# A fused attention and expert layer on one core: routing loop reordered, one index DMA per block

## The chip, the cores and the metric

One Trainium2 chip (trn2), one core of it. The metric is the device time of one execution in microseconds (us), taken from unprofiled runs; the kernel's time is their median. A profiled execution was taken beside them; all views of the trace come from that one.

## What is computed

One decoder layer on 1024 tokens of width 1024, all float32: RMS norm, one combined projection, sliding-window and differential attention, gates, an output projection added to the input, and then a sparse expert network. The part that matters here, from the attention's end on:

```python
x = x + mixed @ w_o
xn = rms_norm(x, ffn_norm_g)
logits = xn @ router_w + router_b              # 1024 tokens, 32 experts
top_vals, top_idx = top_k(logits, 4)
gates = softmax(top_vals)
# each token goes to its 4 experts:
h = xn @ w1[e] + b1[e]                          # w1[e] is 1024 x 2048
g, u = split(h); g = min(g, 7); u = clip(u, -7, 7)
y = (g * sigmoid(1.702 * g) * (u + 1)) @ w2[e] + b2[e]   # w2[e] is 1024 x 1024
x = x + sum over the 4 experts of gate * y
out = rms_norm(x, final_norm_g)
```

## The kernel before

The first 886 us are the attention half; the diff doesn't touch it. The expert half has two stages and a short end.

**Routing (lines 1026 to 1155 on VectorE, 1217 to 1273 on PE, 957 to 980 on ACT, 905 to 914 on POOL).** The 1024 tokens are 8 tiles of 128 (NT = 8). For each tile PE makes the output product in two halves of 512 columns, each 8 products of 128x128 by 128x512 (`out_product`, L1251); VectorE adds them to the input (`residual`, L1052); ACT sums the squares and takes the root (`norm_rms`, L963 and L965); VectorE scales (`norm`, L1065); PE transposes the tile (`turn_xn`, L1224), and ACT and VectorE copy the two halves out of PSUM (`store_xn`, L971 and L1075). PE makes the logits (L1237), VectorE finds the best four and a 0/1 mask (`best`, L1080 to L1093), ACT the exponentials (L975), PE counts the tokens ahead of each in each expert, over all tiles so far (`rank`, L1243), and VectorE turns this into positions (`place`, L1098 to L1107). POOL then scatters, in 4 indirect DMAs per tile, each token's number and gate to its position in a DRAM table of slots, `slot_rows`, where a row has 8 bytes (L912). SP stores the residual and the normalised rows to DRAM.

The order is written out by hand on each engine as a loop over rounds t, each step lagging by a number of rounds. On PE a round is: both halves of tile t, transposes of t-1, logits of t-2, rank of t-3. ACT's exponentials and VectorE's `place` lag four rounds, `best` three. The lists of blocks are computed after the last rank (L1126 to L1155), and end in `list_ready`. SP issues the loads of w2 of expert 0 and of half of w1 of expert 1, 8 MB, after the last tile is stored (L859 and L862).

**Experts.** The slots are cut into blocks of 32 token rows, each of one expert; there are 145 blocks. A block's 32 rows are held in four groups of 32 partitions, each with a quarter of the columns. ACT loads the block's 32 slot rows (`load_slots`, L988) into all four groups of partitions of `idxa`, in four DMAs on its own queue, asked for several blocks ahead, one pair of semaphores `idx_in` for even and odd blocks. POOL adds the group number (L920) and gathers the token rows with an indirect DMA (`gather`, L923), VectorE transposes (L1190), PE makes the product with w1 (`up`, L1283; four k-tiles from `reg_r`, which VectorE copies there for each block, L1183, and four from `w_hi`), VectorE and ACT the activation (L1165 to L1173, L994), PE the product with w2 (`down`, L1306), ACT weighs the rows (L1000), POOL adds them into DRAM (`scatter`, L933). In a block's round ACT does the sigmoid of block n, weighs block n-1 and then issues the index DMAs of block n+4.

SP loads weights as they come free, in loads of 1 MB: when the last block of an expert has used the upper half of w1, the four loads of the next expert's (L868), then the w2 loads (L873) when w2 has been used, and the lower half of w1 of the expert after that (L877).

At the end the rows are read back, normalised and stored.

Of the kernel before, what the change touches and what calls it, by code (L numbers as in the profile page):

```python
# [10 lines left out]
ALU = mybir.AluOpType  # L11
ACT = mybir.ActivationFunctionType
# [686 lines left out]
def expert_half(nc, a, tabs_s, reg_h, reg_r, x_back):  # L699
# [11 lines left out]
    with ExitStack() as ctx:  # L711
# [72 lines left out]
        nb, end_c, count = sm[0:32, 204:205], sm[0:32, 205:206], sm[0:32, 206:207]  # L784
        ntop, exs, rexs = sm[:, 208:216], sm[:, 216:224], sm[:, 224:232]
# [118 lines left out]
        def _(pool):  # L904
# [10 lines left out]
            def gather(n, b, half, reused):  # L915

                pool.wait_ge(idx_in[b], half * 64 + 64)
# [38 lines left out]
        def _(act):  # L956
# [15 lines left out]
            for t in range(NT + 4):  # L972
                if t >= 4:
                    act.wait_ge(top_ready, t - 3)
                    act.activation(ex[:, t - 4, :], top[:, t - 4, 0:TOPK], ACT.Exp, bias=ntop[:, t - 4:t - 3],  # L975
                                   accum_out=exs[:, t - 4:t - 3]).then_inc(ex_ready, 1)
                if t < NT:
                    norm_rms(t)
                if 1 <= t <= NT:
                    store_xn(t - 1)  # L980

            def load_slots(n, b, half):

                if not (isinstance(half, int) and half == 0):
                    act.wait_ge(idx_in[b], half * 64)
                row = act.value_load(listi[0:1, 1, bass.ds(n, 1)], min_val=0, max_val=TABROWS - QB)
                for j in range(NG):
                    act.dma_start(idxa[QB * j:QB * j + QB, bass.ds(n, 1), :].rearrange("p o v -> p (o v)"),  # L988
                                  tab_d[bass.ds(row, QB), :]).then_inc(idx_in[b], 16)
# [28 lines left out]
            act.wait_ge(idx_in[0], n_iters * 64 + 192)  # L1018
            act.wait_ge(idx_in[1], n_iters * 64 + 128)
# [7 lines left out]
        def _(dve):  # L1027
# [17 lines left out]
            def residual(t):  # L1045

                if t == 0:
                    dve.wait_ge(x_back, 16)
                for half in range(2):
                    v = x2[:, t, half * 512:(half + 1) * 512]  # L1050
                    dve.wait_ge(o_proj, 2 * t + half + 1)
                    dve.tensor_tensor(v, v, bank[2 + half][:, :], ALU.add).then_inc(x2_done, 1)  # L1052
# [58 lines left out]
            for t in range(NT + 4):  # L1111
                if 1 <= t <= NT:
                    norm(t - 1)
                if 2 <= t <= NT + 1:
                    store_xn(t - 2)
                if 3 <= t <= NT + 2:
                    best(t - 3)
                if t >= 4:
                    place(t - 4)
                if t < NT:  # L1120
                    residual(t)
# [95 lines left out]
        def _(pe):  # L1217
# [10 lines left out]
            def logits(t):  # L1228
# [5 lines left out]
                if t >= 2:  # L1234
                    pe.wait_ge(rank_taken, t - 1)
# [4 lines left out]
            def rank(t):  # L1240
                pe.wait_ge(mask_ready, t + 1)
                for s in range(t + 1):
# [3 lines left out]
            def out_product(t):  # L1246
                for half in range(2):
                    if t:
                        pe.wait_ge(x2_done, 2 * t - 1 + half)
                    for k in range(KD):  # L1250
                        ins = pe.matmul(bank[2 + half][:, :], mixT[:, k, t * P:(t + 1) * P], wo_s[:, k, half * 512:(half + 1) * 512],  # L1251
                                        start=(k == 0), stop=(k == KD - 1))
                    ins.then_inc(o_proj, 1)
            for t in range(NT + 3):
                if t < NT:
                    out_product(t)
                if 1 <= t <= NT:
                    turn_xn(t - 1)
                if 2 <= t <= NT + 1:
                    logits(t - 2)  # L1260
                if t >= 3:
                    rank(t - 3)
# [89 lines left out]
```

## Time and profile before

| | |
|---|---|
| median of 3 runs | 3001.46 us (2997.08 to 3006.98) |
| profiled execution, its own time | 3002.64 us |
| its span, first to last instruction | 3000.8 us |
| mean granted TensorE clock | 0.931 of full speed |
| busy: PE, VectorE (DVE), ACT, POOL | 88%, 49%, 12%, 24% of the span |
| bytes moved | 499.22 MB in 166005 packets |

A profile page gives each engine's busy time, the span in slices, the DMA queues (q1 is SP's, q10 ACT's, q0 POOL's), the chain of work that ended last, and the costliest groups of instructions, each with the idle time of the engine before it and what ended that. Questions to the trace give the same for a stretch: its instructions in order of time, the DMA packets in it, busy times and granted clock. "L1283" is a line of the kernel. Names such as `reg_r<-in_w` say what is written from what.

### The profile page before, as it was taken

Reading aid. Unit: us, or ns where it says so; the run is one execution under the profiler, and the core shown is the slowest. Engines: PE = TensorE matmul, PEld = TensorE weight load, DVE = VectorE, ACT = ScalarE, POOL = GpSimd, SP = SyncE. Lnnn points to the kernel's source line nnn. Section 1 sums busy time; section 2 is a strip of 40 time slices with the busy share of each in tenths; the row PEclk is TensorE's granted clock in tenths of the full one; section 3 lists DMA queues with packets and bytes.
Section 4 is the critical chain, followed back from the end, with each engine's and each line's share of the span. In section 5 each row is a group of like instructions: output and inputs, shape, how many; then the busy total and the mean of one; then the engine's idle time right before and its main releaser. Section 6 shows DMA issues by size and latency. Waiting matters only on the chain.

```text
span 3000.8 us, 63110 instructions
## 1 busy us (share of the span) xinstructions
PE 2642.1 (88%) x22972; PEld 1187.1 (40%) x22973; DVE 1481.6 (49%) x2879; ACT 364.6 (12%) x870; POOL 724.8 (24%) x623
## 2 busy tenths in 40 slices
PE   8999988899998868799999989899889879997755
PEld 4644666444444422244433424234333323332212
DVE  4342787201114445466666656565555546664334
ACT  2001554100001200000000000000000000000002
POOL 0000000000000323244444424244334333442112
PEclk9998798899999879899999989999999999998878
DMA  3100000500025478731556283935786775579993
GB/s 134 56 28 1 1 1 1 154 28 21 21 86 173 143 245 320 255 119 26 191 179 200 71 306 106 363 113 176 258 296 211 242 273 186 189 249 368 378 355 133
DMA packets 166005, 499.22 MB, mean 166 GB/s; under 512 B 46032, under 2 KB 82384, under 8 KB 132944
## 3 DMA queue, kind: packets, MB, share of 16 engines
q1 hardware_dynamic: 108176, 459.96, 40.8%
q0 software_dynamic: 29168, 38.39, 6.7%
q10 hardware_dynamic: 28608, 0.19, 0.5%
q8 instruction: 29, 0.48, 0.1%
q14 instruction: 24, 0.20, 0.0%
HBM read 466.64 MB, written 32.15 MB: 166 GB/s over the span
## 4 chain that ended last, share of the span: by engine, by line
PE 41%; DMA 26%; issue 1%; SPq 1%; DVE 1%; ACT 0%; DVEq 0%; ACTq 0%; POOLq 0%; POOL 0%
PE xbank L1283 24%; DMA w_hi<-in_w 17%; PE xbank L1306 13%; DMA reg_r<-in_w 9%; PE xbank L1251 3%; PE xbank L1293 1%; PE xbank L1300 0%; DVE reg_h L1213 0%; PE xbank L1237 0%; DMA w_hi<-in_b 0%; SPq L868 0%; DMA reg_h<-acc_rows 0%; PE xbank L1224 0%; SPq L877 0%; DMA acc_rows<-stage,idxs 0%
## 5 line engine op out<-in xcount | busy, mean ns | idle before, releaser
L1183 DVE COPY reg_r<-reg_r 128x2048 f32 x580 | 678.5, 1225 | 467.4 <-DMA reg_r<-in_w 219.5
L1283 PE MATMUL xbank<-reg_r,stage 128*32 128x512 f32 x4640 | 572.5, 630 | 102.6 <-DVE reg_r L1183 81.0
L1306 PE MATMUL xbank<-reg_r,stage 128*32 128x256 f32 x9280 | 561.3, 391 | 79.8 <-DMA reg_r<-in_w 79.4
L1283 PE MATMUL xbank<-w_hi,stage 128*32 128x512 f32 x4640 | 555.2, 613 | 58.4 <-DMA w_hi<-in_w 58.3
L1306 PEld LDWEIGHTS xbank<-reg_r,stage 128*32 128x32 f32 x9280 | 312.5, 113 | 318.1 <-DMA reg_r<-in_w 103.4
L933 POOL DMA_INDIRECT acc_rows<-stage,idxs x145 | 340.9, 2351 | 120.9 <-POOL idxs L930 110.0
L1283 PEld LDWEIGHTS xbank<-reg_r,stage 128*32 128x32 f32 x4640 | 157.9, 114 | 427.6 <-issue 277.1
L1283 PEld LDWEIGHTS xbank<-w_hi,stage 128*32 128x32 f32 x4640 | 153.5, 112 | 393.4 <-issue 261.7
L930 POOL TENSOR_TENSOR idxs<-idxa,tok 128x1 int32<-128x1 int32 x145 | 28.8, 199 | 971.1 <-ACT stage L1000 940.0
L531 PE MATMUL pair<-reg_r,reg_h 128*128 128x512 f32 (+1 forms) x640 | 253.2, 551 | 0.3 <-DMA reg_r<-in_w_in 0.3
L923 POOL DMA_INDIRECT stage<-xn_rows,idxg x147 | 192.8, 1311 | 121.5 <-POOL idxg L920 113.0
L994 ACT ACTIVATE stage<-stage 128x256 f32<-128x256 f32 x145 | 60.5, 417 | 1297.5 <-DVE stage L1165 978.2
L905 POOL DMA_DIRECT2D bcs<-order_table x1 | 0.8, 756 | 886.3 <-POOLq L86 886.3
L920 POOL TENSOR_TENSOR idxg<-idxa,tok 128x1 int32<-128x1 int32 x147 | 205.7, 1400 | 14.5 <-DMA idxa<-slot_rows 13.3
L531 PEld LDWEIGHTS pair<-reg_r,reg_h 128*128 128x128 f32 x640 | 119.3, 191 | 114.6 <-issue 110.5
L1190 DVE STREAM_TRANSPOSE stage<-stage 128x256 f32<-128x256 f32 x147 | 63.1, 429 | 183.9 <-DMA stage<-xn_rows,idxg 183.8
L1000 ACT ACTIVATE stage<-xbank,idxa 128x256 f32<-128x256 f32 x145 | 68.4, 472 | 472.6 <-PE xbank L1306 453.2
L1251 PE MATMUL xbank<-reg_r 128*128 128x512 f32 x256 | 114.2, 605 | 9.4 <-DVE reg_h L1052 7.5
L648 PE MATMUL pair<-reg_h,reg_ka 128*128 128x512 f32 x256 | 114.3, 606 | 4.2 <-DMA reg_r<-in_w_diff_out 4.2
L648 PE MATMUL pair<-reg_h,reg_g 128*128 128x512 f32 x256 | 111.2, 592 | 0.0
L1165 DVE TENSOR_SCALAR stage<-xbank 128x256 f32<-128x256 f32 x145 | 61.4, 423 | 70.5 <-PE xbank L1283 70.3
L283 ACT ACTIVATE reg_r<-pair,small 128x256 f32<-128x256 f32 (+7 forms) x128 | 76.8, 600 | 114.4 <-DVE small L417 58.2
(187 smaller groups left out, 1959.8 us busy)
## 6 DMA issues: line engine op xcount, KB each, us to landing
reg_r<-in_w SPq DMA_DIRECT2D x256, 1024.0 KB
w_hi<-in_w SPq DMA_DIRECT2D x128, 1024.0 KB, 5.6
idxa<-slot_rows ACTq DMA_DIRECT2D x596, 0.2 KB
reg_r<-in_w_in SPq DMA_DIRECT2D x4, 2048.0 KB, 7.9
reg_r<-in_x SPq DMA_DIRECT2D x8, 512.0 KB, 3.4
reg_ka<-in_w_in SPq DMA_DIRECT2D x8, 512.0 KB, 3.8
reg_g<-in_w_in SPq DMA_DIRECT2D x8, 512.0 KB, 3.9
reg_r<-in_w_o SPq DMA_DIRECT2D x1, 4096.0 KB, 17.1
```

The costliest lines, as they stand in the source:

```text
L283: act.activation(probs[u % 2][c][:, 0:n], pair[c][:, 0:n], ACT.Exp, bias=nm[:, s:s + 1], scale=ATT_SCALE, accum_out=lsum[:, s:s + 1]).then ...
L531: ins = pe.matmul(bank[n % 2][:, 0:w], hT[:, k, t * P:(t + 1) * P], wv[:, k, :], start=(k == 0), stop=(k == KD - 1))
L648: ins = pe.matmul(bank[br][:, :], wv[:, k, :], hT[:, k, tok], start=(k == 0), stop=(k == KD - 1))
L920: pool.tensor_tensor(idxg[b][:, :], idxa[:, bass.ds(n, 1), 0], group, ALU.add).then_inc(idxg_ready, 1)
L923: pool.indirect_dma_start(out=xg[b], out_offset=None, in_=xn_parts, in_offset=bass.IndirectOffsetOnAxis(ap=idxg[b][:, :].bitcast(U32), axi ...
L933: pool.indirect_dma_start(out=acc_parts, out_offset=bass.IndirectOffsetOnAxis(ap=idxs[b][:, :].bitcast(U32), axis=0), in_=yrow[b], in_offs ...
L1000: act.activation(yrow[b], y_bank[b][:, 0:DG], ACT.Copy, scale=gate_a[:, bass.ds(n, 1), 1]).then_inc(y_taken, 1)
L1183: dve.tensor_copy(w1k[k], lo_from[:, bass.ds(slot, 1), k, :].rearrange("p o n -> p (o n)")).then_inc(w1_filled[k], 1)
L1190: dve.transpose(xT[b], xg[b]).then_inc(xT_ready, 1)
L1251: ins = pe.matmul(bank[2 + half][:, :], mixT[:, k, t * P:(t + 1) * P], wo_s[:, k, half * 512:(half + 1) * 512], start=(k == 0), stop=(k == ...
L1283: ins = pe.matmul(up_bank[b][QB * c:QB * c + QB, :].rearrange("p (h k q) -> p h k q", h=2, q=QB), xT[b][:, QB * k:QB * k + QB], w1k[k].rea ...
L1306: ins = pe.matmul(y_bank[b][QB * j:QB * j + QB, 0:DG], actT[b][:, QB * k:QB * k + QB], w2r[:, k, j * DG:(j + 1) * DG], start=False, stop=( ...
```

## The change

Three edits, all in the expert half.

*Order of the routing loops.* On PE a round is now: first half of tile t's output product, logits of t-2, second half, transposes of t-1, rank of t-2. `logits` waits for the mask of two tiles before (`mask_ready`), and `rank` has the wait for `rank_taken` that `logits` had. On VectorE a round is: `norm` of t-1, first residual add of t, `best` of t-2, second add, copy of t-1, `place` of t-2. ACT's exponentials lag two rounds. All loops are one or two rounds shorter.

*Square root.* After each exponential of rounds 2 to 7 ACT takes one square root of a constant into a spare column.

*Index loads.* `load_slots` issues one DMA for all four groups, whose source is the 32 rows with a repeated outermost dimension of 4, and the counts that are waited for go by 16 instead of 64.

```diff
+        root_c = sm[:, 207:208]
...
-                pool.wait_ge(idx_in[b], half * 64 + 64)
+                pool.wait_ge(idx_in[b], half * 16 + 16)
...
-            for t in range(NT + 4):
-                if t >= 4:
-                    act.wait_ge(top_ready, t - 3)
-                    act.activation(ex[:, t - 4, :], top[:, t - 4, 0:TOPK], ACT.Exp, bias=ntop[:, t - 4:t - 3],
-                                   accum_out=exs[:, t - 4:t - 3]).then_inc(ex_ready, 1)
+            for t in range(NT + 2):
+                if t >= 2:
+                    act.wait_ge(top_ready, t - 1)
+                    act.activation(ex[:, t - 2, :], top[:, t - 2, 0:TOPK], ACT.Exp, bias=ntop[:, t - 2:t - 1],
+                                   accum_out=exs[:, t - 2:t - 1]).then_inc(ex_ready, 1)
+                    if t < NT:
+                        act.activation(root_c, eps_c, ACT.Sqrt)
                 if t < NT:
                     norm_rms(t)
...
-                    act.wait_ge(idx_in[b], half * 64)
+                    act.wait_ge(idx_in[b], half * 16)
                 row = act.value_load(listi[0:1, 1, bass.ds(n, 1)], min_val=0, max_val=TABROWS - QB)
-                for j in range(NG):
-                    act.dma_start(idxa[QB * j:QB * j + QB, bass.ds(n, 1), :].rearrange("p o v -> p (o v)"),
-                                  tab_d[bass.ds(row, QB), :]).then_inc(idx_in[b], 16)
+                act.dma_start(idxa[:, bass.ds(n, 1), :].rearrange("p o v -> p (o v)"),
+                              tab_d[bass.ds(row, QB), :].unsqueeze(0).to_broadcast([NG, QB, 2])).then_inc(idx_in[b], 16)
...
-            def residual(t):
+            def residual(t, half):
...
-            for t in range(NT + 4):
+            for t in range(NT + 2):
                 if 1 <= t <= NT:
                     norm(t - 1)
-                if 2 <= t <= NT + 1:
-                    store_xn(t - 2)
-                if 3 <= t <= NT + 2:
-                    best(t - 3)
-                if t >= 4:
-                    place(t - 4)
                 if t < NT:
-                    residual(t)
+                    residual(t, 0)
+                if t >= 2:
+                    best(t - 2)
+                if t < NT:
+                    residual(t, 1)
+                if 1 <= t <= NT:
+                    store_xn(t - 1)
+                if t >= 2:
+                    place(t - 2)
...
             def logits(t):
...
                 if t >= 2:
-                    pe.wait_ge(rank_taken, t - 1)
+                    pe.wait_ge(mask_ready, t - 1)
...
             def rank(t):
                 pe.wait_ge(mask_ready, t + 1)
+                if t >= 2:
+                    pe.wait_ge(rank_taken, t - 1)
...
-            for t in range(NT + 3):
+            for t in range(NT + 2):
                 if t < NT:
-                    out_product(t)
+                    out_product(t, 0)
+                if t >= 2:
+                    logits(t - 2)
+                if t < NT:
+                    out_product(t, 1)
                 if 1 <= t <= NT:
                     turn_xn(t - 1)
-                if 2 <= t <= NT + 1:
-                    logits(t - 2)
-                if t >= 3:
-                    rank(t - 3)
+                if t >= 2:
+                    rank(t - 2)
```

## Rows read from the trace of the kernel before

**Rows 1.** The chain that ended last, on the page: shares of the span.

```profile
PE 41%; DMA 26%; issue 1%; SPq 1%; DVE 1%; ACT 0%; DVEq 0%; ACTq 0%; POOLq 0%; POOL 0%
...
PE xbank L1283 24%; DMA w_hi<-in_w 17%; PE xbank L1306 13%; DMA reg_r<-in_w 9%; PE xbank L1251 3%; PE xbank L1293 1%; PE xbank L1300 0%; DVE reg_h L1213 0%; PE xbank L1237 0%; DMA w_hi<-in_b 0%; SPq L868 0%; DMA reg_h<-acc_rows 0%; PE xbank L1224 0%; SPq L877 0%; DMA acc_rows<-stage,idxs 0%
```

**Rows 2.** Busy us (count) of PE, PEld, DVE, ACT, POOL; granted clock, DMA share, GB/s.

```profile
940.00:1020.00 80.00, 80.00 (x278) 42.04 (x278) 29.81 (x103) 19.70 (x35) 15.38 (x16) 1.00 0.40 119
...
1030.00:1035.00 5.00, 3.00 (x20) 2.89 (x19) 2.87 (x14) 0.39 (x2) 3.18 (x4) 0.50 1.01 407
```

**Rows 3.** The chain in order of time: start us, us, what.

```profile
1029.45 20.21 DMA reg_r<-in_w
...
1049.66 19.98 issue
...
1069.64 5.31 PE xbank L1283 x32
```

**Rows 4.** Timeline of the tail: start us, us, engine, line, operation [idle before].

```profile
1021.72 1.87 PE L1237 MATMUL xbank<-rw,stage 128*128 128x32 f32 x16
...
1022.97 1.28 ACT L965 ACT_TABLE_LOAD   x1
...
1024.90 1.67 DVE L1065 SCALAR_TENSOR_TENSOR stage<-reg_h,sm,stage 128x256 f32<-128x256 f32 x4
...
1029.24 3.60 PE L1237 MATMUL xbank<-rw,stage 128*128 128x32 f32 x16 [0.64 <-DVE row_of L1098]
...
1034.42 0.37 DVE L1093 TENSOR_REDUCE maskb<-hot 128x32 bf16<-128x128 f32 x1
...
1043.69 0.17 DVE L1107 CAST posi<-sm 128x4 int32<-128x4 f32 x1
```

**Rows 5.** Timeline of POOL: first and last scatter of tile 7.

```profile
1047.39 0.95 POOL L912 DMA_INDIRECT slot_rows<-tok,posi  x1 [0.30 <-issue]
...
1051.17 0.96 POOL L912 DMA_INDIRECT slot_rows<-tok,posi  x1 [0.31 <-issue]
```

**Rows 6.** DMA packets of 1030 to 1036 us (first row) and 1036 to 1062 us.

```profile
DMA packets 660, 2.45 MB, mean 408 GB/s; under 512 B 64, under 2 KB 64, under 8 KB 659
...
DMA packets 1517, 5.72 MB, mean 220 GB/s; under 512 B 639, under 2 KB 639, under 8 KB 1005
...
q0 software_dynamic: 544, 0.02, 1.5%
```

**Rows 7.** Timeline of ACT's queue and POOL at the first blocks.

```profile
1062.02 9.25 ACTq L988 DMA_DIRECT2D idxa<-slot_rows  x16
...
1065.25 0.18 POOL L920 TENSOR_TENSOR idxg<-idxa,tok 128x1 int32<-128x1 int32 x1 [12.00 <-DMA idxa<-slot_rows]
```

**Rows 8.** Costliest groups, on the page: busy us, mean ns, idle us before.

```profile
L994 ACT ACTIVATE stage<-stage 128x256 f32<-128x256 f32 x145 | 60.5, 417 | 1297.5 <-DVE stage L1165 978.2
```

**Rows 9.** DMA of 1078 to 1082, 1082 to 1090 (two rows), 1476 to 1480, 1480 to 1484.

```profile
DMA packets 217, 1.65 MB, mean 412 GB/s; under 512 B 16, under 2 KB 16, under 8 KB 16
...
DMA packets 578, 2.77 MB, mean 346 GB/s; under 512 B 240, under 2 KB 240, under 8 KB 240
...
q10 hardware_dynamic: 192, 0.00, 1.2%
...
DMA packets 419, 1.60 MB, mean 399 GB/s; under 512 B 29, under 2 KB 29, under 8 KB 419
...
DMA packets 472, 1.11 MB, mean 278 GB/s; under 512 B 201, under 2 KB 201, under 8 KB 472
```

**Rows 10.** SP's queue from 898 to 899 us, and the router load's issues (ns).

```profile
q1 hardware_dynamic: 365, 0.05, 29.3%
...
L836 SPq DMA_DIRECT2D rw<-in_router_w x8: 532/532/5161, 890.5 to 899.3; - x8
```

**Rows 11.** The chain's DMA pieces over 10 us, first and last of 50.

```profile
1078.81 11.23 DMA w_hi<-in_w
...
2914.55 11.41 DMA reg_r<-in_w
```

More of the change, by code:

```diff
@@ L1017, in _ @@
             weigh_y(n_iters * 2, 0)
-            act.wait_ge(idx_in[0], n_iters * 64 + 192)
-            act.wait_ge(idx_in[1], n_iters * 64 + 128)
+            act.wait_ge(idx_in[0], n_iters * 16 + 48)
+            act.wait_ge(idx_in[1], n_iters * 16 + 32)
             for t in range(NT):
@@ L1043, in split_bias @@
                 return dve.tensor_copy(parts[64:96, :], whole[64:96, :])
-            def residual(t):
-                if t == 0:
+            def residual(t, half):
+                if t == 0 and half == 0:
                     dve.wait_ge(x_back, 16)
[L1049 to L1052, printed above, removed]
+                v = x2[:, t, half * 512:(half + 1) * 512]
+                dve.wait_ge(o_proj, 2 * t + half + 1)
+                dve.tensor_tensor(v, v, bank[2 + half][:, :], ALU.add).then_inc(x2_done, 1)
             def norm(t):
@@ L1244, in rank, with out_product @@
                 ins.then_inc(rank_done, 1)
[L1246 to L1253, printed above, removed]
-            for t in range(NT + 3):
-                if t < NT:
-                    out_product(t)
+            def out_product(t, half):
+                if t:
+                    pe.wait_ge(x2_done, 2 * t - 1 + half)
+                for k in range(KD):
+                    ins = pe.matmul(bank[2 + half][:, :], mixT[:, k, t * P:(t + 1) * P], wo_s[:, k, half * 512:(half + 1) * 512],
+                                    start=(k == 0), stop=(k == KD - 1))
+                ins.then_inc(o_proj, 1)
+            for t in range(NT + 2):
+                if t < NT:
+                    out_product(t, 0)
[3 more added lines that the diff above has]
+                    out_product(t, 1)
                 if 1 <= t <= NT:
                     turn_xn(t - 1)
-                if 2 <= t <= NT + 1:
-                    logits(t - 2)
-                if t >= 3:
-                    rank(t - 3)
+                if t >= 2:
+                    rank(t - 2)
             pe.wait_ge(x2_done, 2 * NT)
```

## The prediction

> **What bounds the kernel now.** I read the chain that ended last first: PE is 41% of it and DMA 26%, and the DMA part is two loads of the expert stage, the upper half of w1 (17% of the span) and the lower half or w2 (9%) [rows 1]. From 1079 us on this is one pattern: PE works through the blocks of an expert, and when the expert changes it waits for 4 MB. The first and the last of 50 such DMA pieces of more than 10 us stand in [rows 11]; together they are 742 us. So in this kernel the speed of the DMA engines just after an expert change is on the path, and PE's speed between changes is.
>
> The routing stage (886 to 1070 us), which most of the diff touches, comes in two parts. Up to 1021 us PE has no gap: 80.00 us busy out of 80.00 at the full clock [rows 2]. A new order of the same products gives nothing there. After the last output product there is a tail of 48 us up to the first expert product: the chain shows a weight load until 1049.66, 19.98 us of "issue", and PE's start at 1069.64 [rows 3]. The tail is a relay: last logits, last positions, POOL's scatters, their landing, ACT's index loads, the gather.
>
> **The change, part by part.** *Steady routing.* Each round keeps two half products, logits, transposes and rank, all of it PE's own work. What PE waits for is ready before PE comes to it: logits wait for the mask of two tiles before, which is one round old, and a rank for the mask of its tile, made while the second half product runs. The wait that is new on PE is rank's for the positions of two tiles before; behind it stands the next half product, and those positions are a whole round old too. On VectorE the top-4 search now stands between the two residual adds; behind it are the second add, the copy and SP's stores, none of them needed before that half product ends. Cost 0; the cover is PE's 80 of 80 us. If it were gone, the search (from the end of the logits at 1032.84 to 1034.79, 1.9 us) [rows 4] would show once per tile, 15 us over 8. The square root added beside each exponential moves a table load out of the stretch between a tile's sum of squares and its root; ACT is busy 19.7 of 80 us there [rows 2], so the moved load and the extra root cost 0 for all but the last tiles.
>
> *The tail.* The last half product now has one more logits (1.87 us) and one rank ahead of it, so it ends at 1022.9 instead of 1021.0 [rows 4]. Residual 0.7; squares and root 1.5, as the 1.28 us table load is gone; but VectorE is in the copy and placing of older tiles until 1026.1, so the last normalised tile is ready at 1028.2, against 1026.6. PE meanwhile does logits 6 from 1025.8, at 1.2 GHz as the granted clock stands at 0.50 in this tail [rows 2], so 3.6 us like the row at 1029.24 [rows 4]; transposes 2.0, to 1031.4; the exponential of tile 6 now stands ahead of ACT's last copy and brings a 1.28 us load, so the copy ends at 1033.2; logits 7 to 1036.8; search 1.9, rank 0.4, placing 1.5 (as 1042.35 to 1043.86): positions of tile 7 at 1040.7, against 1043.86 [rows 4]. The gain for POOL is larger: it is backlogged now, it works at four scatters a tile, 1.26 us each, and starts tile 7's 3.5 us after their positions are there, so that the last of them ends at 1052.1 [rows 5]. With a lag of two steps those of tile 5 come at 1026.1 and of tile 6 at 1034, POOL is free at 1039, and tile 7's four end at 1046.1: **6.0 us earlier**.
>
> That is not yet the gain, for the scatters land among 8 MB of weights. Before the scatters arrive the loads run at 408 GB/s, with them at 220 [rows 6]: 5.7 MB took 26 us instead of 14, 0.65 us for each of 18 small DMAs. In the new order about 11 of them meet the loads, which saves 4.5 us, but SP starts the loads 1.6 us later, behind the normalised tile. ACT's index load then still shares the engines with what is left. Between 6.0 (POOL) and 2.9 us (the loads) plus 1.1 us for one issue where four stood before the first gather [rows 7], I take **-5 us**; the ends are +2 (the loads drain no earlier and the index load waits for them) and -11 (nothing holds the index load).
>
> *One index DMA per block.* ACT issues four DMAs of 32 rows now, 0.33 us each and 1.8 us with what lies between; one takes about 0.5 us, like the router loads' median [rows 10]. ACT waits for VectorE 978 us in this stage [rows 8], so 1.3 us less issue is worth 0; nor does the gather wait, as indices are asked for two blocks before. The price is in the DMA engines. When the four index DMAs of a block (192 packets: 128 of 8 bytes and 16 completions each) run beside a weight load, the load drops from 412 to 346 GB/s over 8 us, and in another place from 399 to 278 over 4 us [rows 9]: 1.3 and 1.2 us of load time lost. Spread over 16 engines that is 12 packets an engine, **0.1 us per small packet** and engine.
>
> How will the new one be spread? Its DRAM side is [4, 32, 2] with 4 outermost (a repeat), its SBUF side 128 partitions. The kernel has one DMA of that form: the router weights, [4, 32, 32] into 128 partitions. While their backlog drained alone, the queue filled 29.3% of 16 engines, that is 4.7 engines and not 16, and SP was held 5.16 us at one of the eight issues [rows 10]. I read that as four engines (packets in flight overlap a little). Then a block's load is 32 rows and a completion, 33 small packets on each of four engines and none on twelve. A 1 MB weight DMA spans all engines and is complete when the slowest is. If every small packet costs 0.1 us as now, a load that falls wholly in a stretch costs 3.3 us instead of 1.2.
>
> The Trainium skill states this spreading as a rule ("DMA: Bandwidth & Descriptors", section "Why a DMA increments its semaphore by 16 and not by 1"): the number of engines is the largest up to 16 that divides the outermost sizes of both sides, here 4; its rules for authors warn of a leading repeat by name. The share of 29.3% agrees. The rule speaks against this change; by the opposite reading, all 16 engines, the sum would be that of the faster rival below.
>
> Not all 33 are served inside a stretch PE waits for. Now 12 are served in 4 to 8 us, so 33 need 11 to 20 us beside a load; a stretch is 11 to 13 us long, the index packets begin 3 to 5 us into it, and what is left runs on into the next stretch, where the w2 load starts. I take three quarters, 25 packets: 2.5 us against 1.2, **+1.3 us for each of 50 stretches, all but two of which have exactly one index load: +65 us**, less some 5 for the second half of the double stretches (23 us), which already hold all: **+60 us**. Lower end: only what fits in one stretch, 15 against 12 packets, +15 us. Upper end: 8-byte rows alone carry the cost (0.15 us each, 32 against 8), +3.6 us less the share outside, +125 us. I take +60 since it rests on the nearest rows, those with these very packets.
>
> *Sum.* -5 + 60 = +55 us on the profiled execution (3000.8 us span, 3002.6 us in all); the median of the runs is 1.2 us lower: 3001.5 + 55 = **3056 us**.
>
> **Rivals.** *Faster, by the index DMA (0.20).* The place is the same stretch after an expert change. If the repeat is laid out over 16 engines, an engine has 8 rows and 1 completion: 9 packets against 12, 0.3 us less in 50 stretches, -15 us, and with the tail 2981 us. If it is the completions that hold an engine up, one against four saves 0.9 us each, -45: 2951 us. It decides from fewer than 12 small packets on the worst engine. For it: what an engine does between packets is not in the rows. Against it: the 29.3%, and that weight loads bring their own completions and still run at 412 GB/s.
>
> *Nothing measurable (0.10).* Four engines, but the small packets run in the pauses of the weight queue, or the packet price falls when 32 come in one run: +5 for the loads, -5 for the tail: 3001 us. For it: between the upper w1 and the w2 load the queue thins out. Against it: the 12 packets of now already meet the load in both places read.
>
> *Much slower (0.08).* The worst engines don't get free between two changes: where experts have one or two blocks (the end of the stage has a row of 23 us stretches) 66 packets stand behind each other, indices land late, and ACT, which waits for the load of two blocks before, holds the sigmoid queued behind it. All 33 packets inside, at 0.15 us, 3.8 us more in 50 stretches: 3001 - 5 + 190 = 3186 us at worst, from about 3130.
>
> *The change doesn't do what it says* for the roots: a table load stays ahead of the last root. Worth 1.3 us, within every case.
>
> **How the numbers follow.** Forecast 0.62, its own range 3011 to 3121 (-5 + 15 and -5 + 125). A change of 0.3%, 9 us, is about what the measurement can tell. Slower: 0.62 + 0.08 = 0.70. Faster: 0.20. Same: 0.10. For 8 in 10 the range starts inside the faster case (2985, which leaves out 0.1) and ends at 3130 (leaves out nearly 0.1).
>
> **What would show it.** Right: the ACT queue has about 132 packets per block (128 + 4) instead of 192; beside index traffic the loads fall below 300 GB/s for longer than 8 us; upper w1 and w2 stretches of 13 to 16 us instead of 11 to 13; the table load gone before the last root; POOL's last scatter near 1046; first expert product near 1065. Wrong: 144 packets per block would mean 16 engines; stretches of 10 to 11 us the faster rival. If the first expert product is later than 1070, the tail is misread; if PE has gaps before the last output product, a wait was put on it.

## The result, and the profile after

The changed kernel takes 2977.62 us (median of 7 runs, 2968.22 to 2987.5), the kernel before, on the same chip, 3002.29 (2997.08 to 3007.07). The ratio is 0.9917, 95% interval 0.9894 to 0.9941: 25 us faster, where 55 us slower was forecast. Both the sign and the size are wrong. The profiled execution took 2983.48 us, its span is 2981.6, the mean granted clock 0.931 as before. A later, separate measurement (e11 below) gave 2982.97 us, ratio 0.9922 (0.9900 to 0.9944).

Lines have moved: the upper product L1283 is L1290 now, the lower L1306 is L1313, the logits' L1237 is L1241, the scatter's L912 is L913, the positions' L1107 is L1109. First the page of the changed kernel, the chain by engine and line, and then the row of ACT's queue in its list of DMA queues (packets, MB, share of 16 engines):

```profile
PE 42%; DMA 26%; issue 1%; DVE 1%; SPq 1%; POOL 0%; ACT 0%; DVEq 0%; ACTq 0%; another core or an unknown queue 0%; POOLq 0%
PE xbank L1290 24%; DMA w_hi<-in_w 16%; PE xbank L1313 13%; DMA reg_r<-in_w 8%; PE xbank L1256 3%; PE xbank L1300 1%; PE xbank L1307 0%; DVE reg_h L1217 0%; PE xbank L1241 0%; DMA slot_rows<-tok,posi 0%; DMA w_hi<-in_b 0%; PE xbank L1228 0%; DMA idxa<-slot_rows 0%; POOL slot_rows L913 0%; SPq L869 0%
...
q10 hardware_dynamic: 19668, 0.15, 0.3%
```

The chain has the shape of [rows 1], with the upper w1 at 16% in place of 17 and w2 at 8 in place of 9. 19668 packets are 149 loads of 132: 128 rows of 8 bytes and 4 completions. So the one index DMA does sit on four engines, as forecast; the fact was right and the price on it was not.

**Where the 19 us between the two profiled spans went.** I cut each span at the first output product and at the first expert product. The attention half is 4.0 us shorter (886.3 to 882.3 us; the diff does not touch it, and other kernels of this study with the same code lie between 881.6 and 887.3, so I take it as scatter between executions). The routing half is 6.3 us shorter (183.3 to 177.0), the expert half 8.9 (1931.2 to 1922.3).

*Routing.* PE is as full as in [rows 2] up to the last output product (busy times of a window of 80 us, in the columns of those rows):

```profile
936.00:1016.00 80.00, 80.00 (x290) 42.92 (x288) 32.49 (x110) 25.43 (x45) 19.51 (x20) 1.00 0.36 119
```

The tail, from the timeline of the changed kernel: logits of tile 6 and 7, positions of tile 7, POOL's first and last scatter of that tile.

```profile
1022.01 1.97 PE L1241 MATMUL xbank<-rw,stage 128*128 128x32 f32 x16 [1.79 <-ACT stage L972]
...
1027.00 3.59 PE L1241 MATMUL xbank<-rw,stage 128*128 128x32 f32 x16 [0.60 <-issue]
...
1034.41 0.17 DVE L1109 CAST posi<-sm 128x4 int32<-128x4 f32 x1
1034.85 0.96 POOL L913 DMA_INDIRECT slot_rows<-tok,posi  x1 [0.40 <-DVE posi L1109]
...
1038.64 0.96 POOL L913 DMA_INDIRECT slot_rows<-tok,posi  x1 [0.30 <-issue]
```

With the 4.0 us of the attention half taken off, the positions of tile 7 are 5.3 us earlier than in [rows 4], and the last scatter is 8.5 us earlier than in [rows 5]: POOL is not backlogged any more, it starts 0.3 us behind the positions in place of 3.5. What comes next is two landings (the chain in order of time):

```profile
1038.64 8.34 DMA slot_rows<-tok,posi
...
1047.71 6.89 DMA idxa<-slot_rows
...
1055.80 2.93 DMA stage<-xn_rows,idxg
...
1059.25 6.45 PE xbank L1290 x32
```

15.2 us of the tail are two landings, that of the last scatter (128 rows of 8 bytes) and that of one 1 KB index load, both beside weight loads. Of POOL's 8.5 us, 6.4 arrive at the first expert product (1059.25 + 4.0 against 1069.64 in [rows 3]).

*Experts.* The chain waits for weights 50 times, as before. I sorted its DMA pieces over 6 us into three kinds: the upper w1 of an expert whose predecessor has several blocks ("short w1"), the upper w1 where an expert has one block and both matrices are waited for at once ("long w1", over 20 us), and w2. Each cell is count x mean us, worked out from the chain of waits of one profile; the last column is the stretch from the first expert product to the end. All kernels but the first are described below.

| kernel | short w1 | long w1 | w2 | expert half |
|---|---|---|---|---|
| before | 19 x 11.55 | 12 x 23.57 | 19 x 12.60 | 1931.2 |
| after | 19 x 10.95 | 12 x 23.51 | 19 x 12.64 | 1922.3 |
| e1, four index DMAs | 19 x 11.67 | 12 x 23.12 | 19 x 12.76 | 1937.7 |
| e2, before with one index DMA | 19 x 11.12 | 12 x 23.98 | 18 x 12.50 | 1922.7 |
| e3, after without the root | 19 x 10.97 | 12 x 23.96 | 19 x 12.45 | 1922.2 |
| e4, none beside the weights | 18 x 10.89 | 12 x 22.09 | 17 x 10.59 | (other start) |
| e5, one, sent twice | 16 x 10.92 | 12 x 26.21 | 16 x 12.31 | 1961.0 |
| e6, four, sent twice | 19 x 11.61 | 12 x 23.38 | 19 x 12.81 | 1934.8 |
| e7, two DMAs of 64 rows | 16 x 11.16 | 12 x 24.11 | 15 x 11.46 | 1898.1 |
| e10, four index DMAs again | 19 x 11.76 | 12 x 23.35 | 19 x 12.50 | 1940.5 |
| e11, after again | 19 x 11.13 | 12 x 23.60 | 19 x 12.47 | 1919.6 |
| e12, one, issued earlier | 19 x 11.71 | 12 x 24.40 | 19 x 14.89 | 1999.0 |

From before to after only one column of waits moves: 0.60 us less in each of 19 short waits for w1, 11.4 us. It is the column that sorts the kernels by their index load, too: before, e1, e6 and e10 have 11.55 to 11.76, the four with one index DMA as it stands in the change 10.95 to 11.13.

The means over all profiles of either form say the same with less scatter. With four index DMAs (before, e1, e10) the expert half takes 1936.4 us, with one (after, e2, e3, e11) 1921.7, which is 14.7 us less. 12 us of this are 19 short waits of 0.62 us less. PE's own pieces of the chain are 6.6 us shorter, 5.5 of them by the granted clock (their length times the share of the clock that was not granted is 43.8 us with four DMAs, 38.3 with one), and small pieces of 4 us, mostly of e2's chain, go the other way.

One pair of a short wait for w1 and a wait for w2, before and then after (the chain in order of time, around 1540 us):

```profile
1541.95 11.39 DMA w_hi<-in_w
...
1558.21 12.51 DMA reg_r<-in_w
```

```profile
1527.44 10.55 DMA w_hi<-in_w
...
1542.87 13.01 DMA reg_r<-in_w
```

And the DMA packets of the last 2.6 us of the two waits for w1, with ACT's queue in the second row of each, before and then after:

```profile
DMA packets 204, 0.67 MB, mean 256 GB/s; under 512 B 115, under 2 KB 124, under 8 KB 124
...
q10 hardware_dynamic: 99, 0.00, 1.9%
```

```profile
DMA packets 176, 1.04 MB, mean 401 GB/s; under 512 B 40, under 2 KB 50, under 8 KB 50
...
q10 hardware_dynamic: 24, 0.00, 0.5%
```

The block's index packets meet the weights at the end of the wait. Spread over 16 engines, 99 of them are served in 2.6 us and the weights fall to 256 GB/s; on four engines 24 are served in the same time and the weights keep 401. The rest of the 132 go on after the wait is over, when PE is at work and nobody waits for a weight. The pair is typical: over the 19 short waits the last 2.6 us have 283 GB/s on average before (285, 290 and 277 in e1, e6 and e10), 403 after (395, 402 and 392 in e2, e3 and e11), and 412 in e4, which has no index DMA there.

### The profile page after: what moved, and what is told of

The parts are those of the page before. It is cut to its first block, busy times and chain, and to the rows that moved or that the text cites. A ratio compares the mean times of both kernels' runs of the same rounds, so it can differ in the third digit from the quotient of the medians.

```text
span 2981.6 us, 61800 instructions
## 1 busy us (share of the span) xinstructions
PE 2635.9 (88%) x22972; PEld 1160.6 (39%) x22973; DVE 1479.7 (50%) x2879; ACT 371.1 (12%) x880; POOL 721.7 (24%) x623
## 3 DMA queue, kind: packets, MB, share of 16 engines
q10 hardware_dynamic: 19668, 0.15, 0.3%
## 4 chain that ended last, share of the span: by engine, by line
PE 42%; DMA 26%; issue 1%; DVE 1%; SPq 1%; POOL 0%; ACT 0%; DVEq 0%; ACTq 0%; another core or an unknown queue 0%; POOLq 0%
PE xbank L1290 24%; DMA w_hi<-in_w 16%; PE xbank L1313 13%; DMA reg_r<-in_w 8%; PE xbank L1256 3%; PE xbank L1300 1%; PE xbank L1307 0%; DVE reg_h L1217 0%; PE xbank L1241 0%; DMA slot_rows<-tok,posi 0%; DMA w_hi<-in_b 0%; PE xbank L1228 0%; DMA idxa<-slot_rows 0%; POOL slot_rows L913 0%; SPq L869 0%
## 5 line engine op out<-in xcount | busy, mean ns | idle before, releaser
L1290 PE MATMUL xbank<-reg_r,stage 128*32 128x512 f32 x4640 | 588.0, 644 | 102.3 <-DVE reg_r L1187 83.2
L1313 PE MATMUL xbank<-reg_r,stage 128*32 128x256 f32 x9280 | 548.1, 386 | 82.0 <-DMA reg_r<-in_w 81.9
L1290 PE MATMUL xbank<-w_hi,stage 128*32 128x512 f32 x4640 | 549.7, 608 | 49.2 <-DMA w_hi<-in_w 49.2
L1313 PEld LDWEIGHTS xbank<-reg_r,stage 128*32 128x32 f32 x9280 | 299.3, 112 | 320.6 <-DMA reg_r<-in_w 97.4
L1290 PEld LDWEIGHTS xbank<-reg_r,stage 128*32 128x32 f32 x4640 | 153.5, 116 | 444.9 <-issue 267.5
L1290 PEld LDWEIGHTS xbank<-w_hi,stage 128*32 128x32 f32 x4640 | 147.1, 111 | 385.8 <-issue 265.2
L906 POOL DMA_DIRECT2D bcs<-order_table x1 | 0.8, 758 | 882.3 <-POOLq L86 882.3
L921 POOL TENSOR_TENSOR idxg<-idxa,tok 128x1 int32<-128x1 int32 x147 | 199.0, 1354 | 16.1 <-DMA idxa<-slot_rows 14.1
```

What stands on the lines that cost most here:

```text
L921: pool.tensor_tensor(idxg[b][:, :], idxa[:, bass.ds(n, 1), 0], group, ALU.add).then_inc(idxg_ready, 1)
L1290: ins = pe.matmul(up_bank[b][QB * c:QB * c + QB, :].rearrange("p (h k q) -> p h k q", h=2, q=QB), xT[b][:, QB * k:QB * k + QB], w1k[k].rea ...
L1313: ins = pe.matmul(y_bank[b][QB * j:QB * j + QB, 0:DG], actT[b][:, QB * k:QB * k + QB], w2r[:, k, j * DG:(j + 1) * DG], start=False, stop=( ...
```

## The experiments

### Undo one part each (e1, e2, e3)

e1 is the changed kernel with the index load of before, e2 the kernel before with the new index load, e3 the changed kernel without its added square root.

```
 e1 (from the changed kernel; e2 is the reverse, in the kernel before)
-act.dma_start(idxa[:, n], tab_d[row : row + 32] repeated [4, 32, 2]).then_inc(idx_in[b], 16)
+for j in range(NG):
+    act.dma_start(idxa[32 * j : 32 * j + 32, n], tab_d[row : row + 32]).then_inc(idx_in[b], 16)
 e3
-                    if t < NT:
-                        act.activation(root_c, eps_c, ACT.Sqrt)
```

> The changed kernel with the four index DMAs of before: loops and roots alone. Theory A (the gain is in the tail of the routing stage): 8 to 16 us faster than before, about 2989 us, nearly as fast as the changed kernel within 10 us; expert stage from first expert product to the end as before, 1931 us in its profile. Theory B (the single index DMA brings most of it, by fewer completions for each engine): only 6 us faster than before, 2996 us, and the expert stage unchanged. Theory C (my prediction's price of 0.1 us per small packet holds, and something else hid it): this kernel would be 40 us or more faster than the changed one.

> The kernel before with the single index DMA per block, nothing else. Theory A: 0 to 9 us faster than before, the trace's expert stage 1922 to 1931 us. Theory B: 12 to 20 us faster, expert stage below 1922 us, upper-w1 stretches shorter by 0.5 us each. Theory C: 40 us or more slower. In all of them 132 packets per block on the ACT queue.

> The changed kernel without the square root beside each exponential. A table load of 1.28 us comes back before the root of the last tile, so the last normalised tile may be up to 1.3 us later; VectorE's placing of tile 5 covers most of it (it ended 0.7 us after the root). All theories: 0 to 1.5 us slower than the changed kernel, less than the runs can tell; the table loads in the trace decide.

Measured: e1 3000.17 us, 0.9984 of the kernel before (0.9964 to 1.0004); e2 2990.63 us, 0.9943 (0.9924 to 0.9961); e3 2987.16 us, 0.9929 (0.9906 to 0.9953). So the index load alone brings 17 us (e2) of the 25, and taking it out of the changed kernel loses about 20 (e1); the routing alone brings 5 us, which its interval does not separate from nothing. The square root brings nothing in the whole that can be told from the changed kernel's 0.9917. In the tail it does show: without it the last scatter ends 159.3 us after the first output product, and in the eleven profiles with both the new loops and the root 156.8 to 157.3 us after it. Theory A fell, and theory B's signs and sizes held but for 0.7 us (e2's expert half is 1922.7 us, not below 1922); its reason is looked at next.

### No index loads beside the weights (e4)

All index DMAs are issued ahead of the first sigmoid, in place of one per block in the loop.

```
+load loop: load_slots(i * 2 + (m + 5), 1 - m, i + (2 + m))  for all blocks
 sigmoid(0)
 block loop: sigmoid(n); weigh_y(...)
-            load_slots(i * 2 + (m + 5), 1 - m, i + (2 + m))
```

> The changed kernel with all index DMAs issued before the first sigmoid, so none runs beside the later weight loads. This adds a start of 150 to 300 us in which index loads go one after the other; what counts is the expert stage after it in the trace, from the first sigmoid to the end. If the single index DMA still costs 1 us per stretch that PE waits in (theory A and B), that stage is 30 to 60 us shorter than in the changed kernel; if it costs nothing now, it is the same within 5 us; if it cost what I predicted (2.5 us and more per stretch), 125 us shorter.

Measured: 3236.92 us, ratio 1.0774, since the loop of loads holds the first sigmoid up for 286 us; the waits behind it are what it was run for. From the start of the fourth block to that of the last it takes 1739.2 us, after takes 1827.6, before 1835.7, e1 1840.7. So the one DMA still costs 88 us there, and four cost about 100. Not all of it is waiting: in that stretch of e4's chain the waits for weights are 67 us shorter than the changed kernel's and PE's pieces 38 us shorter, 35 of these by the granted clock, while gathers and small pieces add 16. The waits (one pair of e4's chain):

```profile
1851.45 10.84 DMA w_hi<-in_w
...
1867.17 10.64 DMA reg_r<-in_w
```

Without index traffic a wait for w2 takes 10.6 us in place of 12.6, and a short one for w1 10.9, which is what the changed kernel already has. In w2's wait the index load costs 2.0 us in either form, and in a long wait for w1 about 1.5. The clock goes with w2's wait: after none of e4's 17 is it at 0.5 within the next 10 us, after 14 of the changed kernel's 19 it is, for 2.8 us on average.

### More packets on four engines, and on sixteen (e5, e6)

```
 e5: behind the one index DMA, once more the same
+act.dma_start(idxb[:, 2 * b : 2 * b + 2], the same source).then_inc(idx_in[b], 16)
 e6: behind the four, the four once more, into idxb
```

> The changed kernel with its one index DMA sent twice per block, the second copy into a small tile that nothing reads; all waits count both. Per block 8 small completions and 66 packets on each of 4 engines, in place of 4 and 33. Theory M (what an index DMA costs is set by how many DMAs each engine is given; the one index DMA beside the weight stretches costs about 88 us over the expert half by the experiment that took them away, and four cost about 100): the second copy adds little per packet but one more completion on 4 engines: +5 to +25 us against the changed kernel. Theory P (the packets of the most loaded engine set it, the prediction's step, at the smaller price that 88 us over 33 packets gives): another 33 packets double it, +70 to +90 us. Theory F (a stretch pays once for having an index DMA in it, whatever its size): within 5 us of the changed kernel.

> The changed kernel with the four index DMAs of before, and the four sent again into a small tile that nothing reads: per block 128 completions and 24 packets on each of 16 engines. To be held against the changed kernel with four DMAs (3000 us). Theory M (DMAs per engine): four more on every engine, +50 to +110 us. Theory P (packets of the most loaded engine at 2.7 us for 33): 12 more packets an engine, +25 to +50 us. Theory F (once per stretch, whatever the size): within 5 us of it.

Measured: e5 3023.9 us, 1.0060 (1.0032 to 1.0087), 43 us over the changed kernel; e6 3001.93 us, 0.9992 (0.9973 to 1.0011), against e1's 0.9984 no difference. For e6 theory F held: twice the packets on sixteen engines cost nothing, though all 384 of a block, 24 on an engine, are served inside w2's wait (12.81 us, 12.76 in e1). For e5 no theory was right. Twice the packets on four engines left the short waits and those for w2 as they were (10.92 and 12.31 us), but these are no test of the size: no more packets are served in them than in the changed kernel (34 and 128 on average, against 32 and 114), the rest comes later. The 12 long waits are 2.7 us longer on average. Eight of them start with an index load in service that is served to its end in them, 264 packets in place of 132. These eight are 3.9 us longer, but unevenly, by 0.4 to 7.2 us; the other four, which hold no whole index load, are 0.3 us longer. As an estimate, 3.9 us for 33 more packets on an engine are 0.12 us each. The chain of e5 has two of the longest:

```profile
2701.84 28.65 DMA w_hi<-in_w
...
2743.83 31.11 DMA w_hi<-in_w
```

(e5's chain also has the landing of the index's second copy on it, which the kernel waits for too, 66 us in all, and the gathers behind it, 19.)

### The same rows in two DMAs (e7)

```
-act.dma_start(idxa[:, n], rows repeated [4, 32, 2]).then_inc(idx_in[b], 16)
+for j in range(2):
+    act.dma_start(idxa[64 * j : 64 * j + 64, n], rows repeated [2, 32, 2]).then_inc(idx_in[b], 16)
```

> The changed kernel with its index load as two DMAs of 64 partitions each: the same 128 packets of 8 bytes, two DMAs, each on 2 engines by its shape. If both go to the same 2 engines these carry 66 packets each; if not, it is the changed kernel's load with other names. Theory P (packets of the most loaded engine): +70 to +90 us in the first case, nothing in the second. Theory M (DMAs per engine): one more completion on 2 engines, 0 to +15 us. Theory F (once per stretch): within 5 us. The number of 4-byte completions stays 4 per block in all.

Measured: 2958.93 us, 0.9834 (0.9814 to 0.9854), the fastest kernel of the study: by the ratios 25 us below the changed kernel (19 by the medians, which were taken on two chips), where the theories expected it slower or equal. Its queue has the same 19668 packets. One pair of its waits:

```profile
1589.91 10.86 DMA w_hi<-in_w
...
1605.64 12.07 DMA reg_r<-in_w
...
1617.76 1.07 PE xbank L1314 x16
```

Its waits for w2 are 1.2 us shorter than the changed kernel's, and the clock behind them is better: at 0.5 within the next 10 us after 2 of 15, against 14 of 19. PE's pieces of its chain lose 22 us to the clock, the changed kernel's 42 (e11's 38). It has a price, too: the landing of the index is on its chain for 74.5 us and the gathers for 24, mostly in places where the changed kernel waits for weights, so that the chain has 43 waits for weights in place of 50. In the long waits one block's index packets took some 18 us to be served, against some 10 in the changed kernel, and three of the long waits are 26 to 28 us long. Nearly twice the time for the same packets says that both DMAs use the same two engines; that is inferred, as the trace does not name engines.

### A load of w1 out of the tail's way (e8, e9)

```
-for k in range(4): load next_lo[:, k] (w1 of expert 1, 4 MB)
+sp.wait_ge(list_ready, 1)
+sp.wait_ge(idx_in[0], 32)
+sp.wait_ge(idx_in[1], 32)
+for k in range(4): load next_lo[:, k]
-sp.wait_ge(list_ready, 1)
```

The two counts are those of two index loads each, so the 4 MB go behind the first four index loads, not three.

> The changed kernel with one load of weights moved: the 4 MB of w1 for expert 1, which are issued at 1027 us and run beside the last scatters and the first index loads until 1047, are issued after the first three index loads have landed. Theory T (the landing of the scatters, 8.3 us, and of the index load, 6.9 us, is long because of these bytes): the two take 2 to 4 us each, the first expert product comes 5 to 9 us earlier after the last output product (routing stage 177.0 us, to 168 to 172), and the whole is 5 to 9 us faster if nothing late in the first expert takes it back. Rival T2 (the 4 MB, moved 10 us later, delay the upper w1 and w2 of the next expert by as much): stage shorter, the whole within 3 us of the changed kernel. Rival T3 (the landing is the latency of the scatters themselves): routing stage within 2 us of 177.

> The changed kernel with both edits that came out faster: the index load as two DMAs of 64 partitions, and the 4 MB of w1 for expert 1 issued behind the first three index loads. If the two gains lie in different stretches (theory: the landing of w2 in the expert half, and the landing of scatters and index in the routing half) they add: 2978 - 19 - 6 = about 2951 to 2956 us. Rival: the later w1 meets the later index loads in the first experts, and 2958 to 2965 is left. First expert product 171 to 173 us after the first output product.

Measured: e8 2973.8 us, 0.9894 (0.9870 to 0.9918); e9 2962.94 us, 0.9867 (0.9836 to 0.9898). The tail of e8, in the chain's order:

```profile
1038.16 6.84 DMA slot_rows<-tok,posi
...
1045.72 3.03 DMA idxa<-slot_rows
...
1049.94 3.15 DMA stage<-xn_rows,idxg
...
1053.62 5.50 PE xbank L1292 x32
```

The index load lands in 3.03 us in place of 6.89, the scatters in 6.84 in place of 8.34, and the routing half is 171.6 us, not 177.0, as theory T said (172 in e9). Of its two landings the index's came within 2 to 4 us and the scatters' did not. The later load is paid for in part, as rival T2 said: the first wait for the upper w1 is 16.1 us in place of 11.6. In the whole the gain is not separated from nothing: e8's interval overlaps the changed kernel's, and e9 is not faster than e7 alone, so its rival's range (2958 to 2965) held.

### One engine each, which came out as sixteen (e10)

> The changed kernel with its index load as four DMAs of 32 partitions, each written with an outer dimension of 1, so that by its shape each goes to one engine with 32 packets and one completion. Theory C1 (the fewer engines hold index packets, the less the weights lose, 16, 4 and 2 engines having given 3000, 2978 and 2959; all four on one engine): the landings of w2 shorter again, 0.5 to 1 us each on some 15, but the index itself lands after 30 us or more in the stretches of experts with one block, and the gathers wait for it: 2950 to 2990 us. Theory C2 (four DMAs on four different engines): as the changed kernel's load with three more issues on ScalarE, 2975 to 2985. Theory C3 (the late landing of the index decides): over 3000.

Measured: 3000.73 us, 0.9982 (0.9965 to 1.0000). The row of ACT's queue on its page:

```profile
q10 hardware_dynamic: 28608, 0.19, 0.5%
```

28608 is 149 x 192, the count of the kernel before: the outer dimension of 1 changed nothing, and each DMA went over 16 engines with 16 completions. So the run tests none of the three theories and says nothing of one engine; it is a second e1, and agrees with it (3000.17), short waits for w1 included (19 x 11.76 us).

### The changed kernel again, and the index load issued earlier (e11, e12)

```
 e12
-weigh_y(i * 2 + m, m)
 load_slots(i * 2 + (m + 5), 1 - m, i + (2 + m))
+weigh_y(i * 2 + m, m)
```

> The changed kernel itself, beside the others on one chip: 2978 us, 0.992 of the kernel before, 2972 to 2985. Every other kernel of this call is held against this one too.

> The changed kernel with the index load of a block issued on ScalarE between the sigmoid and the weighing of the last block's rows, in place of behind the weighing: some 4 us earlier in the block, the same packets. In the stretches in which the landing of w2 is waited for, the index packets now come between 3 and 9 us into the wait and beside the gather, and the bytes fall to 270 to 340 GB/s there. Theory E1 (that meeting is what the index DMA costs): the index lands before w2's bytes come, the 19 waits for w2 fall from 12.6 us towards the 10.6 us that they had with no index DMA, 20 to 38 us faster than the changed kernel. Theory E2 (the packets cost the same wherever they meet a load): within 5 us of it, with longer waits for the upper w1. Theory E3 (the issue, 1.1 us, delays the weighing and through it the scatter or the next block): 5 to 15 us slower.

Measured: e11 2982.97 us, 0.9922 (0.9900 to 0.9944); e12 3068.41 us, 1.0222 (1.0196 to 1.0249), 85 us over e11, worse than any theory. A pair of its waits, with what PE did behind the second, and the window behind it (busy us of the engines, granted clock, DMA share, GB/s):

```profile
1542.85 11.43 DMA w_hi<-in_w
...
1559.16 15.43 DMA reg_r<-in_w
...
1574.63 1.93 PE xbank L1313 x16
```

```profile
1574.60:1580.00 5.40, 5.37 (x48) 1.86 (x52) 1.81 (x3) 0.47 (x1) 1.55 (x2) 0.73 0.65 266
```

The index load is issued 3.3 us earlier, and now the packets of two index loads are served in 13 of the 19 waits for w2: one from some 2 us on, and one, issued behind the next sigmoid, from 12.5 us on. These 13 waits take 16.0 us on average, the other six, with few or none of the second load's packets inside, 12.5. With e4 and the changed kernel this is a series: no index load in w2's wait 10.6 us, one 12.6, two 16.0. On the chain the expert half's 77 us over the changed kernel's profile are w2's waits (43 us), the waits for w1 (25) and SP's issues (13), with PE's pieces 6 us shorter.

The row of 1.93 us, in place of e7's 1.07, is the clock behind the wait, which stood at 0.5. But this is not new in e12, the changed kernel has it as well:

```profile
1542.87 13.01 DMA reg_r<-in_w
...
1555.92 1.45 PE xbank L1313 x16
```

In e12 the clock is at 0.5 within 10 us behind 15 of the 19 waits for w2, for 3.0 us on average, in the changed kernel behind 14, for 2.8. e12's mean clock is lower (0.919 in place of 0.931) mostly because it falls inside the waits, where the chain waits for weights and not for PE; PE's pieces of the chain lose 48 us to it, the changed kernel's 42.

## Why the prediction was wrong, point by point

**The chain and the four engines** were right: 50 waits, all of the same two loads, and 132 packets per block.

**Steady routing at 0** was right: PE is busy 80 of 80 us in both. The added root changed nothing in the whole that could be told, as said; in the tail it was worth some 2 us (e3).

**The tail, -5.** The stage gave -6.3 in the profiles and -5 us in e1, whose interval holds zero. POOL's last scatter came 8.5 us earlier, not 6.0. With the 4.0 us added, the last normalised tile was ready at 1028.2, as forecast; but the logits of tile 6 ran at the full clock (1.97 us, not the 3.6 of the working), and the table load ahead of ACT's last copy fell into a time in which ACT waited. So the logits of tile 7 ended at 1034.6, not 1036.8. Of the 8.5 us 6.4 arrived at the first expert product, where the forecast had 5 of 6.0: the landings of scatter and index took the rest.

**The index DMA, +60, is the step that failed.** It measured -17 to -20. Its term was "+1.3 us for each of 50 stretches": 25 packets on the most loaded engine against 12, at 0.1 us each, a price read with the packets spread over sixteen engines and carried over to four. The packets that ACT's queue has inside the waits, from the traces, with the packets of one engine worked out for sixteen engines and for four:

| kernel | inside w2's wait | w2 | inside a short wait for w1 | short w1 |
|---|---|---|---|---|
| before, four DMAs | 192, 12 an engine | 12.60 | 136, 8.5 an engine | 11.55 |
| e6, four sent twice | 384, 24 an engine | 12.81 | 149, 9 an engine | 11.61 |
| after, one DMA | 114, 28 an engine | 12.64 | 32, 8 an engine | 10.95 |
| e4, none | 0 | 10.59 | 0 | 10.89 |

*In w2's waits* the count was right. The packets begin 5 us into them and 28 an engine are served, but the +1.3 us did not come: 12, 24 and 28 packets an engine all cost 2.0 to 2.2 us over none. So there the price per packet of the most loaded engine failed. *In the short waits for w1* the count failed as well: the packets begin 8.5 to 8.8 us into them (7.9 to 8.2 before), in all but the first wait, from which [rows 9] were read (5.0 us, and 4.5 before). So 8 packets an engine fall inside, not 25. Before had 8.5, for which the price gives nothing, and the wait fell by 0.6 us. What goes with it is the rate of all engines together: in the windows shown the weights lose (412 - 256) x 2.6 / 412 = 1.0 us to 6 packets on each of sixteen engines, and 0.07 us to 6 on each of four. *In the long waits*, eight of which start with an index load in service, nothing moved either (23.57 and 23.51). Only e5 showed a cost that grows with the packets on four engines, and unevenly.

Of the 17 to 20 us, 19 x 0.6 = 11 to 12 us are placed in the short waits for w1, and some 5 in the clock of PE's pieces; the rest is spread too thinly to be placed. That the price fails is shown by these counts; why four engines lose less than sixteen in one kind of wait and as much in another is not. The smaller term beside it, 0.5 us for ACT's one issue, was 1.06 and cost nothing, as said.

**The rule of the Trainium skill** ("DMA: Bandwidth & Descriptors", section "Why a DMA increments its semaphore by 16 and not by 1") held for the spreading, with 132 packets a load. Its page's warning against a leading repeat names no price, and as a reason against this change it misled. For a transfer of 1 KB beside 4 MB that somebody waits for, four engines were better than sixteen, and e7's form, on two if the inference holds, was better still. What the narrower form costs shows where the small DMA is itself waited for: its landing is on the chain for 66 us in e5 and 74.5 in e7.

**The rivals.** The faster one had the right sign, but neither branch holds: the first (2981, near the 2978 measured) wants the load on sixteen engines, and it is on four; the second (2951) wants the completions to be what costs, and e6 doubled them on every engine for nothing. That its number came near is luck. The much slower one describes e5, which has its 66 packets: the long waits grew and indices landed late there, for 43 us and not the 130 or more that it gave. **What would show it:** the packets and the root's table load came as named. **The stretches of 13 to 16 us** that the prediction named as its sign did not come; they were 11.0 and 12.6.

**What stays open.** Why w2's wait costs 2.0 us once an index load is in it, on four engines or sixteen, single or doubled; why the short waits for w1 tell four engines from sixteen; why w2 lands 1.2 us earlier beside e7's two DMAs than beside the one; and which engines they use.

## What to carry to other kernels

A small DMA beside a load that is waited for can't be priced as packets on the most loaded engine times a price read at another spreading: here the same 28 packets on four engines and 12 on sixteen cost one kind of wait the same, and in another kind four engines cost less. So find first when in the wait its packets begin, in every kind of wait and not in the first alone, and then try the narrower form: it can be the better choice, as long as the small load itself has a block or two to land. Moving its issue can cost more than any choice of its shape: 3.3 us earlier put two loads into most of w2's waits, and the kernel took 85 us more.

## What the runs showed that I had not expected

- The same 128 rows of 8 bytes gave 3000 us over sixteen engines, 2978 to 2983 over four and 2959 in two DMAs of 64 rows; doubled, they cost 43 us on four engines and nothing on sixteen.
- Four small index DMAs per block held the weights at 256 GB/s in the last 2.6 us of a wait, one DMA at 401; over all 19 such waits the means are 283 and 403.
- The clock behind w2's wait goes with the wait's length: it was at 0.5 (1.2 GHz) within the next 10 us after none of 17 waits of 10.6 us (e4), 2 of 15 of 11.5 us (e7), 9 of 19 of 12.6 us before and 14 of 19 of 12.6 us after. After the short waits for w1 it was there in 9 of 19 cases before and 2 of 19 after.
- In the long waits the clock is at 0.5 for 12 to 18 us, while the chain waits for the weights, and back at full speed behind most of them (9 of 12 before).
- An outer dimension of 1 in the description of a DMA is as if it were not there: 192 packets per block as without it.
